# Opening of the second feed-forward matrix: where SyncE waits, and what it issues behind that wait

## The reference

```
h = rmsnorm(x, norm_ffn)
x = x + jnp.square(jax.nn.relu(h @ w_ffn1)) @ w_ffn2
...
y_prompt = rmsnorm(xp, norm_final)
y_sample = rmsnorm(xs, norm_final)
```

## Time and profile before

| | us |
|---|---|
| median of 3 runs | 1680.87 (1680.84 to 1681.4) |
| the profiled execution | 1680.67 |
| its span in the trace | 1678.7 |
| PE busy in the span | 1630.2 |
| DVE busy | 1165.1 |
| ACT busy | 805.2 |

### The profile page before, as it was taken

One profiled execution on the slowest core, in us unless ns is written; L12 is line 12 of the kernel. 1 busy time (PEld: TensorE's weight loads), 2 busy tenths in 40 slices (PEclk: granted clock), 3 DMA queues, 4 the chain that ended last, 5 costly groups with the idle time before them and its releaser, 6 DMA issues.

```text
span 1678.7 us, 26263 instructions
## 1 busy us (share of the span) xinstructions
PE 1630.2 (97%) x10302; PEld 1452.0 (86%) x10302; DVE 1165.1 (69%) x1762; ACT 805.2 (48%) x1301; POOL 37.6 (2%) x49
## 2 busy tenths in 40 slices
PE   9999999999999989999999999999999999999998
PEld 8877777888999977888988889999999888888886
DVE  7477777666868688556165786666666787777786
ACT  5577777774535367314274533333332343433344
POOL 1000000000000002001000100000000000000001
PEclk9999999999999999999999999999999999999999
DMA  6221322211102252720272224333444863444332
GB/s 205 77 81 55 86 71 61 68 38 40 38 28 67 65 170 78 269 63 26 76 203 72 104 82 145 131 121 127 145 145 164 328 214 122 141 144 155 126 101 113
DMA packets 157691, 190.72 MB, mean 114 GB/s; under 512 B 5505, under 2 KB 117761, under 8 KB 155522
## 3 DMA queue, kind: packets, MB, share of 16 engines
q1 hardware_dynamic: 157570, 189.05, 34.5%
HBM read 134.84 MB, written 54.20 MB: 113 GB/s over the span
## 4 chain that ended last, share of the span: by engine, by line
PE 48%; DVE 3%; issue 1%; ACT 1%; POOL 0%; DVEq 0%; POOLq 0%; ACTq 0%
PE PS L2863 7%; PE PS L2865 7%; PE PS L2864 7%; PE PS L2684 7%; PE PS L2680 7%; PE PS L2682 6%; PE PS L2006 1%; PE PS L2004 1%; PE PS L2005 1%; PE PS L591 1%; PE PS L2106 1%; PE PS L2547 1%; PE PS L2549 1%; PE PS L2548 1%; DVE sbuf_ops_S L2534 0%
## 5 line engine op out<-in xcount | busy, mean ns | idle before, releaser
L629 PE MATMUL PS<-sbuf_h_hi,sbuf_w_hi 128*128 128x384 f32 x600 | 211.4, 352 | 1.2 <-ACT sbuf_g_N L645 1.2
L631 PE MATMUL PS<-sbuf_h_hi,sbuf_w_lo 128*128 128x384 f32 x600 | 201.8, 336 | 0.0
L630 PE MATMUL PS<-sbuf_h_lo,sbuf_w_hi 128*128 128x384 f32 x600 | 201.5, 336 | 0.0
L2863 PE MATMUL PS<-sbuf_ops_w,sbuf_go_u 128*128 128x512 f32 x448 | 174.6, 390 | 2.3 <-DVE sbuf_gg_X L2952 2.3
L2864 PE MATMUL PS<-sbuf_ops_w,sbuf_go_u 128*128 128x512 f32 x448 | 174.3, 389 | 0.0
L2865 PE MATMUL PS<-sbuf_ops_w,sbuf_go_u 128*128 128x512 f32 x448 | 174.3, 389 | 0.0
L2680 PE MATMUL PS<-sbuf_ops_S,sbuf_ops_w 128*128 128x288 f32 x512 | 150.8, 295 | 2.4 <-DVE sbuf_ops_S L2534 1.3
L2684 PE MATMUL PS<-sbuf_ops_S,sbuf_ops_w 128*128 128x288 f32 x512 | 151.1, 295 | 0.0
L2682 PE MATMUL PS<-sbuf_ops_S,sbuf_ops_w 128*128 128x288 f32 x512 | 150.8, 294 | 0.0
L2705 ACT ACTIVATE sbuf_ff_u<-PS 128x576 f32<-128x576 f32 x64 | 41.5, 649 | 168.5 <-DMA uD<-sbuf_ff_sums 97.1
L629 PEld LDWEIGHTS PS<-sbuf_h_hi,sbuf_w_hi 128*128 128x128 f32 x600 | 113.2, 189 | 9.8 <-issue 7.8
(11 more groups left out here) (335 smaller groups left out, 3800.7 us busy)
## 6 DMA issues: line engine op xcount, KB each, us to landing
sbuf_gg_u<-uD SPq DMA_DIRECT2D x28, 1024.0 KB, 5.1
uD<-sbuf_ff_u SPq DMA_DIRECT2D x16, 1152.0 KB, 4.2
sbuf_ff_raw<-w_ffn SPq DMA_DIRECT2D x16, 1024.0 KB, 6.9
sbuf_gg_B<-w_ffn SPq DMA_DIRECT2D x16, 1024.0 KB, 8.1
sbuf_raw<-w_in SPq DMA_DIRECT2D x28, 512.0 KB, 4.6
uD<-sbuf_ff_sums SPq DMA_DIRECT2D x16, 768.0 KB, 6.2
sbuf_X<-x_prompt SPq DMA_DIRECT2D x16, 512.0 KB, 7.3
xD<-sbuf_X SPq DMA_DIRECT2D x9, 512.0 KB, 2.6
```

Of the source, the lines that this page charges most:

```text
L629: pe.matmul(out, hi, h_hi[:, kb, tok], start=kb == 0, stop=False)
L630: pe.matmul(out, hi, h_lo[:, kb, tok], start=False, stop=False)
L631: last = pe.matmul(out, lo, h_hi[:, kb, tok], start=False, stop=kb == KB - 1)
L2863: pe.matmul(out, u_hi, x_hi, start=first, stop=False, skip_group_check=True)
```

## The change

SyncE's list at the opening of the second matrix is changed in two ways. `store_u(LASTU - 1)`, the two DMAs that write unit 14 to `uD`, moves from ahead of blocks B12 and B22 to behind `u_unit(2)`. And ahead of `u_unit(2)` SyncE now waits until both B12 and B22 have landed. Nothing else is changed; PE, DVE, ACT and POOL keep their instructions and their order.

```
             block_unit("B21", 0)
             sp.wait_ge(f_p, FF_AT["P7", LASTU] + 1)
             u_unit(1)
-            store_u(LASTU - 1)
             block_unit("B12", 0)
             sp.wait_ge(f_p, FF_AT["P5", LASTU] + 1)
             block_unit("B22", 0)
+            for x in ("B12", "B22"):
+                sp.wait_ge(g_in[x].sem, g_in[x].n(16))
             u_unit(2)
+            store_u(LASTU - 1)
             for t in (4, 5, 6, 7):
                 stream_back(t)
```

## The result

| | us |
|---|---|
| before, median of 4 runs | 1680.88 (1680.84 to 1681.4) |
| changed, median of 4 runs | 1689.17 (1688.12 to 1691.22) |
| ratio | 1.0049, 95% interval 1.0036 to 1.0062 |
| profiled execution of the changed kernel, its span | 1689.97, 1688.0 |

The changed kernel is slower by 8.3 us, where 9.7 us were forecast.

A forecast was written before the change was run, and what follows sets the result against it. DVE's chain from T3 was taken to pace PE, with the moved store landing late: 1680.67 us of the profiled execution + 9.7 = 1690.4 us, range 1686.9 to 1692.8 us.

The forecast's parts named there:

- What bounds the place: Opening of the second matrix: DVE's gapless chain from T3 to the addition of k = 1, tile 0, paces PE.
- Which wait ends last: At T3: before, the blocks land 3.3 us later than the store; after the change the store is the late one.
- three signs of being wrong: ACT starting token piece 4 before 1330 us, T3 not directly following, or PE making up time behind 1352 us.
- B22 at 1324.1 us: DMA queue: both blocks land 5.4 us after token load 1, at 1324.1 us instead of 1328.8 us.
- B22 a microsecond earlier: DMA queue: B22 might beat the full queue's price by a microsecond, nothing following it, giving 1686.9 us.
- The pair, 12.3 us: Token load 2 and the moved store, from an empty queue: 12.3 us to the store's landing, at 1336.4 us; lower end 9.8 us.
- The shift of 9.7 us: DVE at T3: start moves from 1328.8 to 1338.5 us, and the end moves by the same 9.7 us.
- The low end of the range, 1686.9 us: Whole time with the pair at 9.8 us and B22 landing a microsecond earlier: 1686.9 us.
- Rival B: Opening of the second matrix: only the order counts, the new wait costs nothing; shift 4.7 us, 1685.4 us; chance 0.06.
- Token load 2 and the residual tiles hidden: SyncE's later DMAs: load 2 lands about 1330 us at no cost; tiles 4 to 7 have over 20 us in hand.
- The clock: TensorE may fall to 1.2 GHz in the stall: taken as 0, hidden by 2.26 us ahead of tile 2; at most 1.7 us.
- PE's pauses: PE between 1334 and 1351 us: pauses adding up to some 12 us instead of 2.3 us, none afterwards.

The follow-up runs named there:

- the additions put first: Kernel before with DVE's low parts of pieces 8 and 9 moved behind the additions of k = 1, tiles 0 and 1: 1678.54 us.
- the changed kernel again: The changed kernel itself, unaltered, timed and profiled once more in further runs: 1688.56 us against 1680.99 us.
- the kernel before again: The kernel before, unaltered, profiled a second time: T3 starts 7.67 us after k = 0, span ends 357.63 us after it.
- the order alone: Changed kernel without the new wait; the store of unit 14 still behind both blocks and token load 2: 1684.83 us, ratio 1.0024.
- the wait alone: Kernel before with the wait for B12 and B22 added ahead of `u_unit(2)`, the store in its old place: 1680.69 us, ratio 0.9996.
- the changed kernel with the additions first: Changed kernel with DVE's low parts of pieces 8 and 9 behind the additions of k = 1, tiles 0 and 1: 1689.81 us, ratio 1.0057.

## Why the prediction was right

- **What bounds the place.** Right. DVE's chain from T3 paces PE, and a shift of T3 goes to the end in full; the table shows it over 14 us, and the additions put first show it from the other side.
- **Which wait ends last.** Right. Before, T3 waited for the blocks; now ACT and DVE stand for the store, and the blocks have long landed. None of the three signs of being wrong came: ACT starts at 1336.12 us, T3 follows directly, and PE makes up nothing.
- **B22 at 1324.1 us.** That is 3.9 us after the first matmul of k = 0. Measured: SyncE goes on 2.95 us after it (1324.47 us), and 3.79 us in the changed kernel again. The price of the blocks was right; what had moved is token load 1, the first term of the sum. It took 7.9 us to land in the profile that was read the earlier trace rows, and 6.9 us in the changed kernel:

```profile
sbuf_gg_u<-uD SPq DMA_DIRECT2D x1, 1024.0 KB, 6.9
```

  Issued at 1312.17 us, it landed at 1319.1 us, and 5.4 us for the two blocks give 1324.5 us, as measured. The same load took 6.9 us in the kernel before again, 7.8 us in the changed kernel again, and 6.5 to 7.5 us in the nine other traces. So the profile before was an execution in which this load came late, and the forecast took its microsecond over. Why the load varies is open. The reason given for B22 a microsecond earlier, that nothing follows it, is not what did it: with the store issued right behind the blocks SyncE went on 12.5 us after the issue of token load 1, against 12.3 us in the changed kernel.
- **The pair, 12.3 us.** From the issue of token load 2 to ACT's start it took 11.50 to 11.93 us in the five traces with the same list (11.65 us in the changed kernel). The row taken from the trace before was within 7%; the sum of two prices, 9.8 us, which I held as the lower end, was further off. The estimate by the Trainium skill, "DMA: Bandwidth & Descriptors", section "Anatomy of one DMA", was 8.9 us; these traces don't agree with it for three DMAs in a row.
- **The shift of 9.7 us** was too large: 7.92 us between the two profiles, less by 1.0 us for token load 1, 0.65 us for the pair and 0.13 us for ACT and DVE (1.97 instead of 2.1 us). Set against the kernel before again, whose token load 1 landed after 6.9 us too, T3 moves by 8.90 us, and only the last two terms remain. The low end of the range, 1686.9 us, had room for all three.
- **Rival B, the order alone.** 4.7 us were worked out, 3.7 us measured by time; in the traces T3 moves by 3.6 us against the kernel before and by 4.6 us against it again, with token load 1 at 6.9 us in both. The other part of the loss, 4.3 us (T3 at 16.57 instead of 12.27 us), belongs to the wait, where some 5 us were worked out, but only with the store behind it: the wait alone costs nothing. The prediction's split into two parts holds only in this order, the store moved first and the wait added then.
- **Token load 2 and the residual tiles hidden.** Right: the run with the wait alone shows both late and no loss.
- **The clock.** Taken as 0 with 1.7 us kept for the range. Right for this kernel: it fell for 10 us and cost nothing. The reason given, the pause ahead of tile 2, is shown by taking it away: then it costs 2.2 us at tile 2, of which 1.2 us are left at the end of the trace. The 1.7 us worked out as the most were too little for the place itself: in that trace the low clock held for 6.8 us, not for 3.4 us as in the earlier trace rows. That the cover was just enough, with 0.73 us and 0 us to spare, was partly luck.
- **PE's pauses** add up to 6.5 us in the waits, not to the 12 us I had named. From 13.75 us after the first matmul of k = 0, where k = 1 had begun before, to tile 2 it is 15.9 us instead of the 17.7 us forecast, and for 9.4 us of that PE is busy, mostly at the lower clock, where tiles 0 and 1 had taken 5.7 us before.

## What to carry to other kernels

A store is also a release: before one is moved back in a queue, look up which buffer it reads and who writes that memory next, here two token pieces in the slots of `f_ub[0]`, in front of everything else on DVE. What a wait on the issuing engine costs is read from what is queued behind it there, and from who waits for that: the stop of SyncE was free with the store in its old place ahead of it, and cost over 4 us with the store behind. And where one engine's list paces another, it pays to ask which of its instructions the other waits for, and to put those first.

## What the hardware showed that I had not expected

- The granted clock fell to 0.50 at about 1338 us in the changed kernel; in the 4 us before, PE had worked 1.74 us, and its longest pause was 2.3 us. With 36 small matmuls in the pauses (3.45 us of 4 us busy) it did not fall. In the changed kernel with the additions first PE had worked less, 1.41 us of the same 4 us and 1.55 us of the next 4 us, and the clock fell only at about 1343 us.
- Its price depends on cover: nothing in the changed kernel; where the pause behind it was gone, 2.2 us at the next tile and 1.2 us at the end.
- The same token load took between 6.5 and 7.9 us to land in the thirteen traces, 7.9 and 6.9 us in two profiles of one kernel, and everything queued behind it moved along, up to T3 and the end. Measured differences of a microsecond between kernels of this kind need the trace beside the time, and a price read off one profile can be a microsecond off.
